# RWKV scan: masked triangles one tile earlier, block exchange in a skewed layout, value products ahead of U

## The reference

```
state = state * w_t - (state . kk_t) (kk_t * a_t)^T + v_t k_t^T
y_t   = state . r_t
y     = head_norm(y) * lnx_g + lnx_b + sum(r*k*r_k) * v ;  out = (y * silu(g)) @ w_out
```

## Time and profile before

| | us |
|---|---|
| median of three runs | 3992.38 |
| the profiled execution: its own time | 3994.14 |
| its span in the trace | 3992.3 |
| the scan, from its first instruction to the next stage's first product | 3254.1 to 3737.6 |
| busy over the whole span: PE, DVE, ACT, POOL | 3654.0, 1820.7, 1235.9, 885.2 |

### The profile page before, as it was taken

The page is one execution under the profiler, slowest core; times in us unless marked ns, Lnnn a source line. Parts: engine busy times, 40 slices in busy tenths (PEclk is TensorE's granted clock), DMA queues, the critical chain, the costliest instruction groups (busy, mean ns, idle before and its releaser), DMA issues. The chain is left out here.

```text
span 3992.3 us, 59744 instructions
## 1 busy us (share of the span) xinstructions
PE 3654.0 (92%) x24282; PEld 2128.9 (53%) x24282; DVE 1820.7 (46%) x3610; ACT 1235.9 (31%) x2223; POOL 885.2 (22%) x544
## 2 busy tenths in 40 slices
PE   8999999989989999999899999997998967766898
PEld 3458854445556666644455456443443336766543
DVE  3346642233134444442456237216578855455322
ACT  1137731012245665611311037112222321111124
POOL 0000023420000000043333200432156631222432
PEclk9999999999999999999999999998999988888899
DMA  6000023241232001030422021101355443322400
GB/s 232 21 22 2 2 97 122 77 103 75 104 96 67 25 25 49 2 116 0 163 95 74 0 85 64 42 0 47 144 204 184 146 152 93 86 85 49 160 11 37
DMA packets 268710, 315.21 MB, mean 79 GB/s; under 512 B 120852, under 2 KB 181636, under 8 KB 268054
## 3 DMA queue, kind: packets, MB, share of 16 engines
q1 hardware_dynamic: 268440, 311.39, 23.3%
HBM read 220.13 MB, written 90.95 MB: 78 GB/s over the span
## 5 line engine op out<-in xcount | busy, mean ns | idle before, releaser
L2190 DVE TENSOR_SCALAR_CACHE_REDUCE la_s<-psum 128x512 f32<-128x512 f32 (+1 forms) x384 | 210.3, 598 | 188.6 <-PE psum L2256 188.6
L2163 ACT ACTIVATE la_pT<-psum 128x512 f32<-128x512 f32 x320 | 172.9, 593 | 215.4 <-PE psum L2266 215.4
L968 POOL TENSOR_TENSOR lg_seven_s<-other_columns 128x512 f32<-128x512 f32 x4 | 5.1, 1266 | 887.4 <-POOLq L110 866.9
L2154 ACT ACTIVATE la_s<-la_s,la_negm 128x1280 f32<-128x1280 f32 x128 | 174.6, 1364 | 18.3 <-DVE la_negm L2199 14.6
L2266 PE MATMUL psum<-ident,la_s 128*128 128x128 f32 x1280 | 166.2, 277 | 0.1
L2266 PEld LDWEIGHTS psum<-ident,la_s 128*128 128x128 f32 x1280 | 139.0, 140 | 40.7 <-issue 34.6
L989 PE MATMUL psum<-room,x_rows 128*128 128x512 f32 x320 | 145.6, 598 | 5.8 <-POOL x_rows L968 5.8
L2250 PE MATMUL psum<-la_kT,la_qT 64*128 64x512 f32 (+1 forms) x672 | 143.1, 544 | 7.5 <-DVE la_s L2190 7.5
L968 POOL TENSOR_TENSOR wg_seven_s<-other_columns 128x512 f32<-128x512 f32 x5 | 6.3, 1270 | 592.6 <-POOLq L110 544.5
L2277 PE MATMUL psum<-la_pT,la_v 128*64 128x128 f32 x2240 | 134.6, 275 | 0.8 <-ACT la_pT L2163 0.7
L833 DVE CUSTOM_DVE_ANT_0 wa_s<-psum,window_mask_rows 128x640 f32<-128x640 f32 (+1 forms) x128 | 100.6, 786 | 71.5 <-PE psum L888 71.5
(11 more groups left out here) (708 smaller groups left out, 8109.4 us busy)
## 6 DMA issues: line engine op xcount, KB each, us to landing
x_rows<-rwkv_raw SPq DMA_DIRECT2D x40, 512.0 KB, 4.6
room<-rwkv_raw SPq DMA_DIRECT2D x33, 512.0 KB, 5.1
later_slot<-in_ada_w_dram SPq DMA_DIRECT2D x16, 1024.0 KB
rwkv_raw<-x_rows SPq DMA_DIRECT2D x64, 256.0 KB, 2.9
rwkv_raw<-x_rows SPq DMA_DIRECT2D x32, 512.0 KB, 3.7
room<-in_odd_w_in_dram SPq DMA_DIRECT2D x6, 2048.0 KB, 13.5
room<-in_even_w_in_dram SPq DMA_DIRECT2D x5, 2048.0 KB, 11.3
ada_slots<-in_ada_w_dram SPq DMA_DIRECT2D x8, 1024.0 KB, 9.2
```

Source lines behind the costliest of these rows:

```text
L2154: act.activation(s_sb[:, g % 2, j, :], s_sb[:, g % 2, j, :], ACT.Exp, bias=negm[:, g % 2, j:j + 1], accum_out=total[:, g % 2, j:j + 1]).th ...
L2163: act.activation(pT[:, h, at * BANK:(at + 1) * BANK], pT_banks[turn], ACT.Copy).then_inc(pT_moved[turn], 1)
L2190: dve.tensor_scalar(s_sb[:, g % 2, j, cols], s_banks[j][:, 0:cols.stop - cols.start], SCALE, NEG, ALU.mult, ALU.max, accum_out=smax[:, g % ...
```

## The change

In the scan, by engine:

- **PE**: tile i+2's quads stand at the end of tile i, after `within`, and use banks 0, 1, 4, 5. `weigh_started` follows `weigh_removals` directly. The v half of `to_state` becomes `values_to_state`, put ahead of the wait for U; the v half of `within` becomes `within_values`, ahead of the second chunk's `to_state`.
- **DVE**: tile i+2's masks stand at the end of tile i; `A` gets a fourth slot. The variances of the tile before come after the seventh join instead of after `make_u`.
- **ACT, POOL**: `norm_heads` comes ahead of the HmT move, and the multiplication by `lnx_g` ahead of the one by the deviation.
- **SP**: `load_blocks` stores two whole 64x64 triangles per chunk (all heads) in rows of 64 floats, and reads the diagonal blocks with a row pitch of 65 times 16, so that every block begins where a row of the view begins. `place_blocks` writes blocks into two zeroed planes with the same view and reads whole planes back, four DMAs. `diagonal` now lies in the room of a dead weight tile. `place_blocks` comes last in the loop, behind the store of the finished tile.
- Before the loop, two tiles are turned, multiplied and masked instead of one, and the planes are cleared.

In the row work, POOL's k row comes after its b row and overwrites `back` instead of `t1`; SP loads the next k and a after the k row.

```diff
     def sp_k_row(self, sp, i):
         sp.wait_ge(self.q["k_row_made"], i + 1)
-        sp.dma_start(self.raw[1][self.at(i), :], self.t1).then_inc(self.q["k_stored"], 16)
+        sp.dma_start(self.raw[1][self.at(i), :], self.back).then_inc(self.q["k_stored"], 16)
         if i + 1 < X_TILES:
-            sp.wait_ge(self.q["bonus_rows"], i + 1)
             self.sp_load_k(sp, i + 1)
+            self.sp_load_a(sp, i + 1)
...
                     if tile is not None:
-                        scan.pool_k_row(pool, tile)
                         scan.pool_bonus(pool, tile)
                     seven.pool_s3(pool, j, pa, pb)
                     if tile is not None:
                         scan.pool_x_row(pool, tile)
                         scan.pool_b_row(pool, tile)
+                        scan.pool_k_row(pool, tile)
...
+                plane = lambda n, c: scan.blocks[n, :, c * C * (C + 1):c * C * (C + 1) + C * C].rearrange("h (r t) -> r h t", t=C)
+                cells = lambda n: scan.blocks[n].rearrange("h (q s) -> (h q) s", s=B * (C + 1))
+                corners = lambda n: cells(n)[:, 0:B * C].rearrange("q (j t) -> q j t", t=C)[:, :, 0:B]
...
                     for u, small in enumerate((small_t, small_x)):
-                        sp.dma_start(scan.blocks[1 + u].rearrange("n h j t -> (n h) (j t)"), small[:, 0:B * B]).then_inc(q["small_out"], 16)
+                        sp.dma_start(corners(1 + u), square(small)).then_inc(q["small_out"], 16)
...
-                    for n in range(BLOCKS):
-                        at_row, at_col = slice(n * B, (n + 1) * B), slice(n % 4 * B, (n % 4 + 1) * B)
-                        for u in range(2):
-                            sp.dma_start(diagonal[at_row, u, :, at_col], scan.blocks[1 + u, n].rearrange("h j t -> j h t")).then_inc(q["diagonal_in"], 16)
+                    for u in range(2):
+                        for c in range(CHUNKS):
+                            sp.dma_start(diagonal[chunk(c), u, :, :], plane(1 + u, c)).then_inc(q["diagonal_in"], 16)
...
                         if m == SUM_AT and i:
                             output_sums(i - 1)
-                    ahead = i + 1 < NT
-                    if ahead:
-                        for n in range(QUADS):
-                            mask_quad(i + 1, n)
+                        if m == VAR_AT and i:
+                            variances(i - 1)
                     make_u(i, 0)
-                    if i:
-                        variances(i - 1)
                     state(i, 0)
...
                     state(i, 1)
+                    if i + 2 < NT:
+                        for n in range(QUADS):
+                            mask_quad(i + 2, n)
...
                     inverse(i)
                     weigh_removals(i)
+                    weigh_started(i)
                     ahead, later = i + 1 < NT, i + 2 < NT
-                    if ahead:
-                        quad(i + 1, 0)
-                    weigh_started(i)
-                    if ahead:
-                        for n in range(1, QUADS):
-                            quad(i + 1, n)
                     from_state(i, 0)
+                    values_to_state(i, 0)
...
+                    within_values(i)
                     if ahead:
                         to_state(i, 1)
-                    within(i)
+                    within_removals(i)
+                    if later:
+                        for n in range(QUADS):
+                            quad(i + 2, n)
                     if ahead:
                         started(i + 1)
```

More of the change, by code:

```diff
@@ L3992, in _ @@
                         scan.sp_b_row(sp, tile)
+                        scan.sp_k_row(sp, tile)
                     if j == 2:
@@ L4431, in rwkv_scan @@
         xT, bT, kT = sb("xT", [P, 2, PAIRS, 2, P]), sb("bT", [P, PAIRS, P]), sb("kT", [P, PAIRS, P])
[L4433 removed]
+        A = sb("A", [P, 4, H, 2, C])
         inv, Z = sb("inverse", [P, 2, H, C]), sb("Z", [P, H, C])
         T, TT = inv[:, 0, :, :], inv[:, 1, :, :]
[L4436 removed]
+        diagonal = scan.pair.rearrange("p (u h t) -> p u h t", u=2, h=H)
         padded = B * (B + 1)
@@ L4517, in _ @@
                 sp.wait_ge(q["zeroed"], 1)
+                for u in range(2):
+                    sp.dma_start(cells(1 + u), scan.pair[:, 0:B * (C + 1)]).then_inc(q["cleared"], 16)
+                sp.wait_ge(q["cleared"], 32)
                 place_blocks(0)
@@ L4547, in _ @@
                         load_gates(i)
+                    if i + 1 < NT:
+                        place_blocks(i + 1)
+                sp.wait_ge(q["joined"], (NT - 1) * UNITS + GROUPS)
                 sp.wait_ge(q["stored"], (NT - 1) * 16)
@@ L4759, in _ @@
                 start.end()
-                for n in range(QUADS):
-                    mask_quad(0, n)
+                for i in range(2):
+                    for n in range(QUADS):
+                        mask_quad(i, n)
                 steps = small_steps_of(0)
@@ L4913, in from_state, with values_to_state @@
                             last.then_inc(q["y_state"], 1)
+                state_out = lambda h: core.banks(2)[at(h), (h // 2) * N:(h // 2 + 1) * N]
+                def values_to_state(i, c):
+                    rows = chunk(c)
+                    for h in range(H):
+                        pe.matmul(state_out(h), k[i % 3][rows, head(h)], v[i % 2][rows, head(h)], start=(h < 2), stop=True, skip_group_check=True)
                 def to_state(i, c):
@@ L4918, in to_state, with within, within_values, within_removals @@
                     for h in range(H):
[L4919 to L4921 removed]
+                        last = pe.matmul(state_out(h), b[i % 3][rows, head(h)], U[rows, h, :], start=False, stop=True, skip_group_check=True)
                     last.then_inc(q["s_prod"], 1)
[L4924 removed]
+                def within(i, u, right):
+                    for h in range(H):
+                        for c in range(CHUNKS):
+                            last = pe.matmul(core.banks(6, 2)[chunk(c), split(h)], A[chunk(c), 2 + i % 2, h, u, :], right[chunk(c), h, :],
+                                             start=False, stop=True, skip_group_check=True)
+                    return last
+                def within_values(i):
                     pe.wait_ge(q["y_state"], (i + 1) * CHUNKS)
+                    within(i, 1, heads(v[i % 2]))
+                def within_removals(i):
                     pe.wait_ge(q["u_moved"], (i + 1) * CHUNKS)
[L4927 to L4939 removed]
+                    within(i, 0, U).then_inc(q["y_prod"], 1)
+                for i in range(2):
+                    for n in range(ITEMS):
+                        turn_rows(i, n)
+                    for n in range(QUADS):
+                        quad(i, n)
                 started(0)
@@ L4959, in _ @@
                     from_state(i, 1)
+                    if ahead:
+                        values_to_state(i, 1)
                     if later:
```

97 lines of the change are left out of this document (39 added, 58 removed).

## The result

The changed kernel takes 3897.17 us (median of four runs, 3893.44 to 3901.36); the kernel before, beside it, 3993.89. The ratio is 0.9759, 95% interval 0.9742 to 0.9776. The forecast was 3900, in a range from 3855 to 3950. In the two profiled executions the span fell from 3992.3 to 3896.7, by 95.6 us.

What follows compares the result with a forecast made beforehand. The inverse's wait for its diagonal blocks, behind the small steps and SP's DMAs, bounds the kernel. Six intervals -69, first interval -8, end -13, beginning +3.5, projections -5: -91.5 from 3994.1 gives 3902.6, median about 3900, range 3855 to 3950.

Steps and rivals of the forecast that it cites:

- J to T: Steady tile, blocks joined (weigh_removals starts) to end of small steps: 18.3 us, 20.3 with 2.0 for PE's issue; before 31.2.
- T to z: Steady tile, end of small steps to next inverse's start, SP's DMAs putting blocks back: 11.6 us against 12.2 before.
- The allowance of 2.0 us for PE's issue: Every tile, behind the joining of blocks: 2.0 us added for PE issue stalls like the last tile's 2.92 us.
- The rival that built on it (3923): All tiles: PE's issue sets the pace, make_u 9.5 us after blocks are joined, as in the last tile; 3923, chance 0.12.
- z to J: Steady tile, start of the inverse to all blocks joined (weigh_removals starts): kept at 13.4 us, bounds 11.2 to 14.5.
- The sum of 45.3: Steady interval between inverse starts: 33.7 to the end of small steps plus 11.6 back, 45.3 us, 11.5 below 56.8.
- The values ahead of U: State update in each tile: PE does the values' half, about 1.0 us, before U, leaving only the U half, 1.0.
- The end: Last tile to next stage: store and reload of normalised rows come earlier, 45.2 to 32 us after the inverse's start, -13.
- The projections: Before the scan: x row no longer behind the k row, five PE waits 1.0 us shorter each, -5, bounds 0 and -27.
- The beginning: Before the first small steps: second tile turned, multiplied and masked ahead, partly covered by idle DVE, +3.5, bounds 0 and 8.
- The slower rival: Way back of blocks: small DMA pieces cost 55.4 ns each, 20.6 us more per tile, 4044; decided above 41 ns; chance 0.05.
- PE's end of the tile: Rival: quads, masks and started at half clock take 17.6 us, not 9, outlasting the DMAs by 6; 3942, chance 0.10.

Runs made afterwards that it cites:

- the first two experiments: Early finishing (variance, norm_heads, POOL's multiplications) undone in the changed kernel: 3935.83 us; the same early finishing alone added to the kernel before: 3952.22 us.
- the run with the weights later: Changed kernel with the next stage's 4 MB of weights loaded behind the reload of the heads, not in the last tile: 3905.78 us, ratio 0.9784.
- with two queues: Changed kernel with the old way back (long-row stores, sixteen block reads), one kind of block on SP and one on ACT: 3868.17 us, ratio 0.9688.

## Why the prediction was right, step by step

- **What bounds the kernel.** Right: the inverse waits for its blocks in every tile, before and after, and both J to T and T to z lie on the path. The sign for this wait, 5 us or less, held at the six starts between (0.52 to 4.49 us) and not at the first tile (16.8) and the last (10.75).
- **From J to T, 18.3 without the allowance.** Right: 18.0 in the third tile, with `make_u`, the state and `small_first` within 0.4 us of their terms. That POOL slows the small steps was argued then and is shown now, in both directions, by the first two experiments; the whole early finishing is worth 39 us.
- **The allowance of 2.0 us for PE's issue.** Wrong: J to T is 18.1 on the mean, so nothing of it is there. It was read from the last tile and spread over all; the run with the weights later shows that the stall there belongs to a 4 MB load that runs only beside the last tile. The rival that built on it (3923) falls with it.
- **From T to z, 11.6.** Mis-sized: 13.1. The two prices held (9.8 ns, and 263 GB/s where 272 was taken). In the third tile the stores took 5.85 us where 4.8 stood, and the reads 7.15 where 6.8 stood. The issue of the two stores took 1.34 us, not 0.4, but that alone is not the miss: in the first tile it took 1.30, the reads started within the 4.8, and T to z was 12.1. What the longer tiles have besides is the packet of the "instruction" queue; whether it is the cause stays open. The prediction's -0.6 a tile is not there: it set 11.6 against the third tile's 12.2, and the means are 13.1 and 12.9.
- **From z to J, 13.4.** 14.1: the last join is 0.6 later for the variance (1.15 against 0.51 of idle time before the removals), and two of six tiles hold issue waits of 2.37 and 1.61 us inside the inverse.
- **The sum of 45.3 was met by luck, because these errors cancel**: +0.7, -2.2 and +1.5. The six intervals gave -71.6 and not -69 because the prediction took 45.3 from the third tile's 56.8; from the mean of 57.3 it would have been -72.
- **The values ahead of U** stood in the sum with PE's 1.0 us taken from behind U. Putting them back moved nothing that could be told from noise.
- **The end, -13**: -10.4, since the stall of the last tile stayed; without it the run with the weights later has -14.5 (30.7 instead of 45.2). **The projections, -5**: -7.8, and the mechanism is only half the one told; the waits fell by 14.5 us, the products behind them took 604 instead of 875 ns each, and more than half of the waits was given back in a later wait for DVE (from 5.4 to 15.7 us), as was nearly all that the products gained, in slower products behind that wait (673 instead of 601 ns). **The beginning, +3.5**: +5.1.
- **The slower rival** needed 41 ns a piece; 9.8 were measured. **PE's end of the tile** does not set the pace after the change (PE idles 0.52 to 4.49 us before the six inverses between the first and the last); with two queues it does so before three of these six.

Of the gain of 97 us the early finishing holds 39, the triangles with the new cutting out 36 when alone (the two were not run apart), the row work 9; the way back and the v halves nothing that could be told from noise. That makes 84. Some of the rest is what the two large parts give each other: triangles sooner put the small steps further under POOL's work (9.3 us instead of 7.2 in half of the tiles), unless that work is done by then. The remainder is not assigned.

## What to carry to other kernels

Look for slow small instructions, and for what another engine does at that very time: moving POOL's work by some microseconds was worth as much as moving all the quads and masks. When SP issues many DMAs in a row on the path, a second queue can be worth more than fewer and larger transfers: here 31 us for the sixteen small reads (3899 to 3868), and nothing measurable for the four large ones. A stall seen in one tile only may have a cause in that tile alone; look for it before it is spread over all.

## What the runs showed of the hardware

A copy of 8 elements per partition took 0.17 us alone and 2.33 us when it began inside a POOL operation of 2.83 us, with which it ended (3410.96 and 3411.00). DVE operations of which one input lies in PSUM kept their time beside POOL: `make_u` took 1.21 us in both kernels, alone in the kernel before (3430.16, POOL from 3433.17) and beside POOL in the changed one (3401.39, POOL's third operation from 3400.30 to 3402.66). This fits the Trainium skill, "SBUF — State Buffer", section "Who interferes with whom", by which DVE and GpSimd share a port pair, and an instruction with one SBUF input only, outside some modes, does not need it.

Four plane reads of 64 partitions each, issued one behind the other, moved at 263 GB/s together from 3425 to 3427. The Trainium skill, "SBUF — State Buffer", section "Can I just issue two DMAs to hit both halves?", says that two such transfers, one at partition 0 and one at partition 64, serialize, with 6% more than one alone. The rate for one, 196 GB/s, which the prediction took, stands in the section on Door 1 of that page of the Trainium skill; the runs do not show that limit here. The 7.2 us worked out from it came close to the measured 7.15 by luck: SP issued the reads over 3.55 us, and behind that they moved faster. With the planes shared between two queues, the engines moved 239 to 243 GB/s.

Beside a load at 403 GB/s PE stood 2.0 us in "issue", and the granted clock was 0.56 from 3624 to 3628; without the load there was no such wait, and the clock was 1.00 from 3622 to 3626.

One packet of 16 KB on the "instruction" queue went with about 1 to 3 us more from the first store of a way back to its first read: 4.48 without and 5.36 to 7.25 with it in the changed kernel, 2.19 to 2.89 and 4.41 to 4.85 in the kernel before. No run isolates it.
